# The first two products behind a norm, made together row by row in two banks

## The reference, cut to what matters

```python
# first network, each layer
h = rms_norm(x, norm_w[layer])
proj = jnp.einsum('bsd,de->bse', h, w_in[layer])     # dt and forget gate, q, k, v, ...
...
y_c = forgetting_attention_branch(c_q, c_k, c_v, c_f, c_z, f_bias[layer])
x = x + jnp.einsum('bsd,de->bse', merged, w_out[layer])
# second network, each layer
h = modulate(rms_norm_2(x, norm_mix[l]), sh1, sc1)
k, v, q, u, f, gt = jnp.split(h @ w_in[l], IN_SPLITS, axis=-1)
...
hf = modulate(rms_norm_2(x, norm_ffn[l]), sh2, sc2)
x = x + g2 * conv_ffn(hf, w_up[l], conv_w[l], w_down[l])
```

## Time and profile before

| | us |
|---|---|
| runs of the kernel before | 2203.31, 2205.13, 2207.19 (median 2205.13) |
| the profiled execution, first to last instruction (span) | 2201.0 |
| the profiled execution's own device time | not given apart from its span |
| median of the runs less the span | 4.1 |
| TensorE busy | 2086.7 (95%) |
| VectorE, ScalarE, GpSimd busy | 1224.0, 1112.0, 959.5 |
| mean granted TensorE clock | 0.978 |
| share of TensorE, VectorE, ScalarE in the chain that ended last | 76%, 11%, 7% |

### The profile page before, as it was taken

How to read it: one execution, slowest core, us unless ns; L and a number is a source line. 1 busy time by engine, 2 the same in 40 slices (tenths; PEclk the granted TensorE clock), 3 DMA queues, 4 the chain that set the end, 5 groups by cost and what they waited for, 6 DMA issues and landing times.

```text
span 2201.0 us, 36805 instructions
## 1 busy us (share of the span) xinstructions
PE 2086.7 (95%) x14870; PEld 1857.8 (84%) x14870; DVE 1224.0 (56%) x2034; ACT 1112.0 (51%) x1892; POOL 959.5 (44%) x424
## 2 busy tenths in 40 slices
PE   6999998999999998999999998999999989999997
PEld 6998997998898998988676786778888867898997
DVE  5587655345577654463365335545544545756565
ACT  5575575544585485554475233433333346646553
POOL 4655644653546554652111332423323333365663
PEclk9999999999999999999999999999999989999998
DMA  6354543565554543654222444333333333354551
GB/s 238 148 192 173 182 152 111 195 214 204 203 188 154 182 155 124 202 187 175 69 87 77 141 145 169 110 124 125 115 134 107 133 115 106 121 180 141 192 182 58
DMA packets 93321, 330.65 MB, mean 150 GB/s; under 512 B 10080, under 2 KB 13408, under 8 KB 92896
## 3 DMA queue, kind: packets, MB, share of 16 engines
q1 hardware_dynamic: 93152, 328.30, 43.2%
HBM read 327.08 MB, written 1.18 MB: 149 GB/s over the span
## 4 chain that ended last, share of the span: by engine, by line
PE 76%; DVE 11%; ACT 7%; issue 2%; DMA 2%; POOL 1%; SPq 0%; DVEq 0%; ACTq 0%; POOLq 0%
PE ps L878 21%; PE ps L880 20%; PE ps L879 20%; ACT t_hi L1239 2%; PE ps L932 2%; DVE t_lo L1554 2%; PE ps L891 1%; PE ps L892 1%; PE ps L893 1%; DMA t_A<-cu_scratch 1%; PE ps L1150 1%; DVE t_B L1742 1%; POOL t_lo L2021 1%; PE ps L1022 1%; PE ps L1006 1%
## 5 line engine op out<-in xcount | busy, mean ns | idle before, releaser
L2021 POOL TENSOR_TENSOR t_lo<-t_raw,t_hi 128x1024 fp32r<-128x1024 f32 (+1 forms) x360 | 884.6, 2468 | 1074.7 <-ACT t_hi L1239 1057.9
L878 PE MATMUL ps<-t_RB,t_hi 128*128 128x256 f32 (+1 forms) x3712 | 1171.0, 315 | 17.8 <-DVE t_RB L1842 5.2
L879 PE MATMUL ps<-t_RB,t_hi 128*128 128x256 f32 (+1 forms) x3712 | 1148.9, 310 | 0.0
L880 PE MATMUL ps<-t_RB,t_lo 128*128 128x256 f32 (+1 forms) x3712 | 1148.2, 309 | 0.0
L878 PEld LDWEIGHTS ps<-t_RB,t_hi 128*128 128x128 f32 x3712 | 712.4, 192 | 91.0 <-issue 32.1
L879 PEld LDWEIGHTS ps<-t_RB,t_hi 128*128 128x128 f32 x3712 | 713.1, 192 | 34.8 <-issue 1.9
L880 PEld LDWEIGHTS ps<-t_RB,t_lo 128*128 128x128 f32 x3712 | 712.3, 192 | 35.6
L1239 ACT ACTIVATE t_hi<-t_raw 128x1024 fp32r<-128x1024 f32 (+1 forms) x506 | 524.5, 1042 | 420.7 <-PE ps L880 386.4
L1554 DVE TENSOR_TENSOR t_lo<-t_raw,t_hi 128x1024 fp32r<-128x1024 f32 x146 | 209.9, 1438 | 285.7 <-ACT t_hi L1239 285.6
L1980 DVE SCALAR_TENSOR_TENSOR t_A<-ps,t_V,t_A 128x510 f32<-128x510 f32 (+1 forms) x176 | 102.2, 612 | 153.7 <-ACT t_A L1514 152.2
L1514 ACT ACTIVATE t_A<-ps,t_V 128x512 f32<-128x512 f32 (+1 forms) x88 | 48.5, 577 | 126.6 <-PE ps L880 126.6
(11 more groups left out here) (295 smaller groups left out, 2153.6 us busy)
## 6 DMA issues: line engine op xcount, KB each, us to landing
t_raw<-in_W SPq DMA_DIRECT2D x586, 512.0 KB, 3.5
t_A<-cu_scratch SPq DMA_DIRECT2D x8, 512.0 KB, 6.4
t_B<-cu_scratch SPq DMA_DIRECT2D x8, 512.0 KB, 4.5
t_raw<-in_W SPq DMA_DIRECT2D x16, 256.0 KB, 2.8
t_A<-in_C SPq DMA_DIRECT2D x2, 1536.0 KB, 6.9
t_X<-in_X SPq DMA_DIRECT2D x2, 512.0 KB, 4.4
t_X<-in_X SPq DMA_DIRECT2D x1, 1024.0 KB, 10.0
out<-t_X SPq DMA_DIRECT2D x1, 1024.0 KB, 4.8
```

The costliest lines, as they stand in the source:

```text
L878: mm(o, hi[:, w], xh(k), start=k == 0 and j == 0, stop=False)
L879: mm(o, hi[:, w], xl(k), start=False, stop=False)
L880: i = mm(o, lo[:, w], xh(k), start=False, stop=k == nkt - 1 and m == u.x[1] - 1)
L2021: tt(t.lo[s][:, 0:w], t.raw[r][:, 0:w], t.hi[s][:, 0:w].bitcast(F), ALU.subtract).then_inc(*up("pool", ("split", u.i)))
```

## The change

Five places of the list are touched: the starts of both layers of the first network, and in the second network the products `uf` of the last layer and `up` of pair 0 in both layers. At each, the first two units of products become one: TensorE makes rows 0 to 5 of both, row by row, each in its own bank, then rows 6 and 7 of the first, then rows 6 and 7 of the second. In the first network the two are `small` and q0, so q0's tick disappears; in the second network's first layer they are the two banks of one product.

```diff
+    def wide(self, l, parts, tw):
+        group, chunks = [], []
+        for kind, c, fn, ncol, x, then in parts:
+            i = self.chunk(8 * ncol, fn)
+            chunks.append(i)
+            for m0 in range(0, max(1, ncol // 128), 512 // tw):
+                group.append((Unit(kind, l=l, c=c, i=i, g=(self.bank(),), x=x(m0), led=True), then, m0))
+        self.add("wide", l=l, x=tuple(u for u, _, _ in group))
+        halves = [(i, h) for i in chunks for h in range(-(-self.width[i] // HF))]
+        self.split_after(*halves.pop(0))
+        for u, then, m0 in group:
+            if then:
+                then(m0)
+            self.units.append(u)
+            if halves:
+                self.split_after(*halves.pop(0))
+        for i, h in halves:
+            self.split_after(i, h)
...
     def small(self, l):
-        i = self.chunk(1024, small_cols(l))
-        self.split_after(i, 0)
-        self.add("small", l=l, i=i, g=(self.bank(),))
-        self.split_after(i, 1)
+        self.wide(l, [("small", 0, small_cols(l), 128, lambda m: (), None),
+                      ("q", 0, wcols("w_in", l, O_QC + np.arange(256)), 256, lambda m: (0, 2), None)], 256)
...
             self.add("s1", l=l, x=(1, t))
+            self.early_split()
             b = self.rstd(t, (2, 1, 1))
             self.add("norm2", l=t, g=b, x=range(8))
             self.late_splits()
-            for c in range(2):
-                self.uf(l, c, self.uf_chunk(l, c), 0, True)
+            self.wide(l, [("uf", c, wcols("w_in_2", l, 768 + np.arange(c * 256, c * 256 + 256)), 256, lambda m: (0, 1), None)
+                          for c in range(2)], 256)
...
         self.add("s1", l=l, x=(4, t + 1))
+        if last:
+            self.early_split()
...
+            first = () if pr else range(512 // tw if last else 1)
+            if pr == 0:
+                self.wide(l, [("up", 0, wcols("w_up_2", l, vg * DFF + np.arange(256)), 256,
...
+    def wide(u):
+        for k in range(6):
+            for v in u.x:
+                led[v.kind](v, ks=(k,))
+        for v in u.x:
+            led[v.kind](v, ks=(6, 7))
```

More of the change, by code:

```diff
@@ L409, in layer1 @@
         for g in range(4):
-            for off, kind in ((O_QC, "q"), (O_KC, "k")):
+            for off, kind in ((O_QC, "q"), (O_KC, "k"))[not g:]:
                 self.gemm(kind, l, g, wcols("w_in", l, off + np.arange(g * 256, g * 256 + 256)), 8, 256, 256)
@@ L571, in block2 @@
             g, p2 = (pr + 1) // 2, (pr + 1) % 2
-            for vg in range(2):
+            first = () if pr else range(512 // tw if last else 1)
+            if pr == 0:
+                self.wide(l, [("up", 0, wcols("w_up_2", l, vg * DFF + np.arange(256)), 256,
+                               lambda m, vg=vg: (m, min(2, m + 512 // tw), vg),
+                               lambda m, vg=vg: self.up_then(l, 0, vg, m, tw)) for vg in first], tw)
+                self.tick()
+                self.mod_turn()
+            for vg in range(len(first), 2):
                 self.gemm("up", l, pr, wcols("w_up_2", l, vg * DFF + np.arange(pr * 256, pr * 256 + 256)), 8, 256, tw,
@@ L867, in taken, with chan @@
             i.then_inc(*up("pe", ("used", u.i + k * ncol // HF), *events))
-    def chan(u, nkt, ncol, tw, xh, xl, point, *events):
+    def chan(u, nkt, ncol, tw, xh, xl, point, *events, ks=None):
         b = gbank(u)
-        for k in range(nkt):
+        for k in ks or range(nkt):
             q.wait_ge(point(k))
@@ L881, in chan, with toks @@
             taken(u, i, k, nkt, ncol, ("mm", u.i, u.x[0]), *events)
-    def toks(u, nkt, ncol, c0, nc, xh, xl, blocks, point, part):
+    def toks(u, nkt, ncol, c0, nc, xh, xl, blocks, point, part, ks=None):
         b = gbank(u)
-        for k in range(nkt):
+        for k in ks or range(nkt):
             q.wait_ge(point(k))
@@ L943, in mod2, with of_h, small @@
         i.then_inc(*up("pe", ("modt", u.l, u.c), ("mtr", u.l * 24 + u.c)))
-    def of_h(u, *events):
-        chan(u, 8, 256, 256, hh, hl, lambda k: at("h", u.l, k), *events)
-    def small(u):
+    def of_h(u, *events, ks=None):
+        chan(u, 8, 256, 256, hh, hl, lambda k: at("h", u.l, k), *events, ks=ks)
+    def small(u, ks):
         b = gbank(u)
-        for k in range(8):
+        for k in ks:
             q.wait_ge(at("h", u.l, k))
@@ L1078, in wout, with uf @@
         chan(u, 8, 256, 256, hh, hl, lambda k: at("m", u.l, k // 2), ("layer", u.l))
[L1080 removed]
+    def uf(u, ks=None):
         z, nz = u.x
         toks(u, 8, 256, 0, 256, block(t.H2), block(t.HL2), (2 * z, 2 * z + 1),
[L1083 removed]
+             lambda k: at("h", 8 if u.l == 0 and z else 3 + 2 * u.l, k), z, ks=ks)
     def k2(u):
@@ L1196, in tensor @@
     todo = dict(rstd=rstd, rstdb=rstdb, mod=mod, mod2=mod2, q=of_h, k=of_h, conv=of_h, rope=of_h, z=of_h, gate=lambda u: of_h(u, ("gatemm", u.l)),
-                small=small, small4=small4, vc=vc, vb=vc, scores=scores, turn=turn, pv=pv, ssm0=ssm0, ssm3=ssm3, ssm4=ssm4,
+                wide=wide, small4=small4, vc=vc, vb=vc, scores=scores, turn=turn, pv=pv, ssm0=ssm0, ssm3=ssm3, ssm4=ssm4,
                 rope2=rope2, gn_sum=gn_sum, proj=proj, wout=wout, uf=uf, k2=k2, v2=v2, q2=lambda u: of_h2(u, 256 if u.l else 512),
@@ L1200, in tensor @@
                 pair4=pair4, proj2=proj2, wout2=wout2, up=ffup, down=down)
+    led = dict(small=small, q=of_h, uf=uf, up=ffup)
     for u in units:
-        if u.kind in todo:
+        if u.kind in todo and not u.led:
             todo[u.kind](u)
```

5 lines of the change are left out of this document (3 added, 2 removed).

## The result

| | median, us | lowest to highest | profiled span |
|---|---|---|---|
| before | 2203.84 | 2201.61 to 2207.19 (5 runs) | 2201.0 |
| after | 2197.84 | 2193.53 to 2199.39 (5 runs) | 2191.8 |

The ratio is 0.9967, with a 95% interval of 0.9955 to 0.998: faster by 6.0 us by the medians and 7.3 by the ratio. The span of the profiled execution is 9.2 us shorter; it is the fastest of the five. I read first where the two traces drift apart. The offset of an instruction is its start in one trace less the start of the same instruction in the trace of before; the table has the median offset of ScalarE's instructions, and by how much it grows over a stretch (times of before, us).

A forecast was written before the change was run, and what follows sets the result against it. TensorE, busy 95% of the span, was taken as the bound, losing time to gaps and half clock behind norms. Terms -4.0 - 4.0 + 1.2 - 2.5 + 2.0 = -7.3 took 2205.1 to 2198 us; range 2189 to 2205.

The forecast's parts named there:

- Up and uf: Second network, up of first layer and uf of last: fewer matmuls behind row 7, -4.0 us each.
- Last up: Second network, last layer's up: interleaving gives 0.4 at most, early split and low clock cost; sum +1.2 us.
- The hold: Ahead of the last layer's up, GpSimd's early split holds VectorE's 0.42 us instruction to near 2 us: +1.6.
- First layer: First network: TensorE stands for q0's weights, and the chain of small comes later; +2.0 us, bounds -3 and +6.
- the stand after the third matmul: First network, first layer: TensorE stands 3 us there, until q0's first half is split at 18.7.
- Second layer: First network: group 1's read back, `fox_prep` and the end of TensorE's stall come earlier; -2.5 us, bounds 0 and -5.5.
- Its first part: First network, second layer: with rows interleaved, TensorE is 5.4 us ahead at q0's end.
- Mods: A `tick` and `mod_turn` fewer in each first-network layer shift where mods stand; costed at 0, +-1.
- A: Alternating banks holds the clock at 1.2 GHz through each wide unit, 3 to 5 us per norm: 2213; chance 0.03.
- B: Full gains everywhere, as the attention's chains do not bind: sum -18, 2187 us; chance 0.10.
- C: First network keeps nothing: first layer +4, second -0.5; last `up` +2, other two norms -7: 2203.6; chance 0.20.
- D: Chain of small decides: first layer's cu at 55 or later, first layer +9, second +3: 2211 us; chance 0.07.

The follow-up runs named there:

- the last experiment: Changed kernel with first layer in turn, last up as before, context's loads behind the last read back, and one more `mod_turn` behind small: 2186.57 us, ratio 0.9925.
- the third experiment: Changed kernel with one more `mod_turn` behind small, giving all mods but one their old places: 2195.82 us, ratio 0.9967.
- the first experiment: Changed kernel with its plan kept, but TensorE makes all eight rows of one product, then of the other, in every wide unit: 2202.88 us, ratio 0.9992.
- The second: Changed kernel without the early split ahead of the last up's norm; the split stands behind the norm again: 2193.4 us, ratio 0.9947.
- the fourth experiment: Changed kernel, but in the first network's first layer TensorE makes small and then q0, plan kept: 2189.32 us, ratio 0.9934.
- seventh: Changed kernel, but TensorE makes small and then q0 in both layers of the first network, plan kept: 2196.31 us, ratio 0.9968.
- sixth: Changed kernel with the loads of the second network's context and constants moved behind group 3 of the second layer's attention: 2190.96 us, ratio 0.9937.
- the joined kernel: Changed kernel with three edits: first layer in turn, context's loads behind group 3, last up as before the change: 2187.48 us, ratio 0.9921.

## Why the prediction was right, and where its terms were not

The forecast of 2198 was met at 2197.84. The gain behind the norms of the second network came by the mechanism that was forecast. That the total fits to 0.2 us is luck. The forecast started from a median of 2205.13, and with two more runs the kernel before has 2203.84: the change was forecast at -7.3 and is -6.0 by the medians. And terms that were off made up for each other: in the profiled execution, the fastest of its five, they sum to -9.3 instead of -7.3, and the first network was forecast at -0.5 and gave -4.7, the second at -6.8 and gave -4.6.

**Up and uf.** Priced at -4.0 each. Over a whole stretch the mods' places and scatter are mixed in: up's stretch gives -2.8 in the kernel after, -4.1 with only these norms, -3.9 in the last experiment and -6.15 in the third. So I read the offset just ahead of row 7 and just behind the products: from 1300 to 1380 against 1393 to 1420 for up, and from 1770 to 1788 against 1796 to 1815 for uf. Either place gives -4.0 to -4.1 in each of the ten kernels that interleave it, and 0.0 in the one that makes it in turn. For up this is the earlier trace rows as counted, 18 x 0.23 = 4.1; for uf it is a little less than 36 x 0.12 = 4.3.

**Last up.** Priced at +1.2, measured +2.6 in four kernels and +1.2 in one (the third experiment), and -0.3 to 0.1 in the four that leave it as it was. The hold was there: 1.7 to 1.8 us for 0.42 in all six kernels with the early split, and the norm's rows come 1.45 late. In turn (the first experiment) that is the whole cost, +1.4. Interleaved, the rest goes with the clock. In the kernel after 27 matmuls start 0.21 apart, from 1981.37 until about 1987.3, where 16 did before; 11 more at 0.21 instead of 0.12 cost 1.0. In the third experiment it was 13, and the interleaving cost nothing. The second, without the hold, has 22 of them and the stand of 0.79, and costs +1.15. So the term was short of the clock, within its bound, and the interleaving won nothing here, as forecast. The Trainium skill says in SBUF — State Buffer, SBUF: two separate sides, that a VectorE operation with two inputs in SBUF and a GpSimd operation that reads SBUF take one shared pair of ports by turns, each for its whole length. The 0.42 alone and 1.80 beside a split agree.

**First layer.** Priced at +2.0, and every step came, the forecast in brackets: the stand after the third matmul of 2.51 (3), cu at 52.3 (51.1), no wait at `small4`, the split at 67.4 (67.7), a stand in q2 of 3.67 (5), and the wait at 88.46 nearly gone. One price was short: behind the first stand 28 matmuls start 0.21 apart, until 24.6, and not 18, which is 0.9 us. The four kernels with this order have +1.9, +1.3, +6.0 and +5.2, a mean of 3.6; five that make it in turn with the same plan have -0.6, -4.6, -3.0, -2.6 and -1.2, a mean of -2.4. So interleaving a product whose weights are late costs some 6 us in the mean against leaving it out, and the ratios of the kernel after and of the fourth experiment are 7 us apart. The plan's part alone seems to be a gain, which I had not priced. That the kernel after shows the forecast's +2.0 almost to the tenth is luck, as the four kernels of this order go from +1.3 to +6.0.

**Second layer.** Priced at -2.5, measured -6.65 in the kernel after; the term is the one mis-sized. Its first part was right: at q0's end all interleaved kernels are 5.0 ahead of before (5.4 forecast), the two in turn 0.3 or less. The chain behind it was not. All times here are in us behind the layer's first row, from the traces:

| kernels | loads of weights ahead of group 1's read back | cu ends | that read back takes | the stand ends |
|---|---|---|---|---|
| before | 7 | 32.3 | 12.1 | 77.9 |
| only the two norms inside the second network | 7 | 31.3 | 12.1 | 76.6 |
| in turn (first and seventh experiments) | 5 | 38.2, 37.8 | 9.9, 10.1 | 76.7, 77.2 |
| interleaved (after, second and fourth) | 5 | 34.6 | 9.7, 9.8, 10.3 | 72.2, 73.1, 73.6 |
| interleaved, old places of the mods (third) | 7 | 34.6 | 12.3 | 77.0 |
| interleaved, context late (sixth) | 5 | 34.6 | 7.0 | 70.2 |
| interleaved, context later, old places of the mods (last) | 7 | 34.6 | 7.1 | 70.4 |

I had said that cu does not move; it ends 2.2 later, and so `fox_prep` of group 0 came only 1.4 sooner (priced 2.7). But SyncE got from there to group 1's read back 1.8 sooner, and that DMA landed 2.35 sooner because five loads of weights since SyncE's last wait were ahead of it and not seven. I had followed the queue of instructions on SyncE and not the bytes in front of the read back. The five come from the mods' new places, as the third experiment shows, and not from the interleaving: there the stand ends only 0.9 sooner than before, and the layer wins 0.1. With the five loads the layer gives -6.65, -4.4 and -4.2 interleaved, and -0.5 and -0.65 in turn. The means are 4.5 apart; the rest of the 6.65 is scatter. So it took both the interleaving and the shorter queue, and the forecast's 2.5 for the queue of before did not come in the one trace that has it.

Moving the context's loads shows that what is in front sets the read back: 9.8 and 7.1 for group 1, 11.1 and 5.9 for group 3. Nor is it a sum of bytes alone: with the context out of the way, seven loads of weights give 7.1 us and five 6.8 to 7.4, and the two loads cost their 2.35 only together with the context's 1.92 MB. The Trainium skill says in DMA: Bandwidth & Descriptors, Queues, rings and completion order, that each DMA engine takes a queue's descriptors in the order of its ring; these landings agree.

**Mods.** Costed at 0, +-1. With up's 4.1 taken off, their new places cost 1.3 in the stretch with up in the kernel after, and 2.1 in turn, where nothing is to be taken off. They also take the two loads from in front of the read back, a gain in the second layer. The third experiment gives both back and has the same ratio as the change.

**Rivals.** A, the swinging clock, is out: in the last wide unit the granted clock rises once, from 0.50 to 1.00 between 1986 and 1988, and stays, with 19 matmuls in the 2 us from 1988. In the other four the distance of the starts also goes from the low level's to the high one's once, at 24.6, 509.4, 1376.4 and 1772.3, and stays there. B held in part (no stand left at 580 once the context moved). C's first layer (+4) came true in two executions with +5 and +6, its second (-0.5) in the third experiment alone (-0.1), whose queue is that of before. D did not come: cu at 52.3.

**Left open.** Why one execution of a program gains or loses 2 to 5 us in the first network; see below. Whether the mods' old places win 1 to 2 us in the median. For whom TensorE stands at 623.21 in the joined kernel.

## What to carry to other kernels

Interleave two products behind a norm only where both have their weights before the first row; the gain was then the matmuls that no longer stand behind the last row, and nothing in the last up, where rows came as fast as TensorE took them. Where a DMA is on the critical chain (here a read back of 512 KB), look at the bytes queued ahead of it, and move loads that nobody needs yet behind it. A split on GpSimd was not free where VectorE had the next link of the chain: it cost 1.45 us.

## What was not expected of the hardware

The same instructions gave different first layers. The in-turn kernel and the one with only the first layer in turn have one program up to 502 us, yet 0.4 us of difference at the first matmul (15.33 and 14.94) has become 4.1 at 500. Clock by stretch of both, first the in-turn one (us, busy time of TensorE, its weight loads, VectorE, ScalarE and GpSimd, granted clock, DMA share, GB/s):

```profile
140.00:170.00 30.00, 27.47 (x236) 26.36 (x236) 24.70 (x38) 22.76 (x44) 11.14 (x4) 1.00 0.47 168
200.00:230.00 30.00, 27.82 (x219) 24.88 (x218) 25.28 (x27) 13.78 (x22) 18.32 (x8) 0.94 0.56 201
```

```profile
140.00:170.00 30.00, 30.00 (x258) 28.82 (x257) 21.39 (x35) 23.30 (x45) 10.51 (x4) 1.00 0.42 152
200.00:230.00 30.00, 27.95 (x235) 25.78 (x234) 26.48 (x30) 14.25 (x23) 18.29 (x8) 1.00 0.57 204
```

In the first stretch TensorE stands 2.5 us in the one and not at all in the other. In the second both stand some 2 us, but only the first has a granted clock below 1.00. Three more kernels have this same program in the first layer, and the five span -0.6 to -4.6 there. A term that is read from one execution over a whole layer of this network is thus good to some 2 to 4 us only, and the medians of four to ten runs have to carry the verdict; read close around a norm, the ten kernels agree within 0.1.
